# A two-layer encoder with 32 experts per layer: half as many, twice as long products per expert, and each expert's down product ahead of the next gate and up products in three rounds of four

## The chip, the core and the metric

The kernel runs on one core of a Trainium2 chip. The metric is the device time of one execution in microseconds (us), the median of several runs. A core has a matrix engine (TensorE, PE in the rows, its weight loads PEld), a vector engine (VectorE, DVE), a scalar engine (ScalarE, ACT), GpSimd (POOL) and a sync engine (SyncE, SP), which here issues the transfers from the chip's memory. All engines run side by side and wait for each other on semaphores. PSUM is the memory that TensorE writes to, in banks of 128 partitions by 512 floats.

## The reference

```python
for l in range(DEPTH):                       # 2 layers, 256 tokens, D_MODEL 1024
    x = x + concat(diff_attention, sparse_attention, mla)(rms_norm(x) @ w_in) @ w_out
    x = x + hier_moe(rms_norm(x))
return rms_norm(x)

def hier_moe(x):                             # 32 experts, 2 chosen per token
    gate, expert = top-2 experts of the best of 4 groups, for each token
    for each expert e, on its tokens xb:
        h = silu(xb @ w_gate[e]) * (xb @ w_up[e])      # 1024 x 512, 1024 x 512
        y = h @ w_down[e]                              # 512 x 1024
    return sum over a token's two experts of gate * y
```

All of it is float32. Every expert's three matrices, 6 MB together, are read from the chip's memory in each layer: 64 times 6 MB, which is most of what the kernel reads.

## The kernel before

One function, `trunk`, holds a program for each engine. In each of the two layers an attention part comes first, then a router, then the experts.

**The experts.** They come in `ROUNDS` = 4 rounds of `BODY` = 8. Each expert has `CAP` = 32 places for tokens. Four experts are a quad, and for each quad `tokens(q)` gathers the tokens by a product with a 0/1 matrix `pick` (line 1748), and ScalarE copies the result into `xg` in eight copies. One expert then is, in the words of this document:

- **P, the gate and up products** (`products`, `gate_up`, line 1766): 32 matrix products with 256 moving columns. The stationary operand has only 32 columns, so four products go side by side to the four groups of 32 columns of the array. The result is in `gu_ps`, 128 partitions by 256.
- ScalarE copies it to `h_rows` (`products_out`, `gu_read`).
- **T, the turning products** (`turned`, `turns`, lines 1777 and 1779): two transposes give h and two small products give the gate-weighted scatter matrix of this expert.
- ScalarE takes an exponential (`exponent`, line 819), and VectorE makes silu(gate) * up in four steps (`hidden`, lines 1230 to 1233, `hid_ready`), then four copies of the scatter matrix (line 1236, `pgt_read`).
- **D, the down product** (`down_of`, line 1789): 16 products of 256 columns into `tr`. ScalarE copies it to `y` (`y_out`, `wide_read`), and in the same place tells SyncE that the down matrix's buffer is free (`d_used`).
- **A, the scatter** (`add`, `scatter`, line 1799): 8 products of 256 columns, four side by side on four groups of 32 rows, add y to the sums of all tokens, which stand in the banks `pj` and `lg`.

TensorE runs its program strictly as written. Before, the order in a round is P(e), D(e-1), T(e), A(e-1).

**The transfers.** SyncE issues all large transfers in one fixed order. The experts' matrices have three places (`PLACES`), each 6 MB, and one late place for two experts of a layer. Experts 0 to 3 of a layer are loaded during the attention part, because their space is free then. Expert 4 goes to the place of expert 0 in pieces, expert 5 to that of expert 1, and from expert 6 on nearly each expert is one transfer of 6 MB (line 570, "all"), expert e into the place of expert e-3: 6 follows the expert 2, 7 the expert 4 (which had the place of 0), 8 the expert 5. Such a transfer waits for both `gu_used` and `d_used` of its place:

```python
if kind != "d":
    sp.wait_ge(gu_used[i], at(l, FILLS[i], uses(i, e)))
if kind != "gu":
    sp.wait_ge(d_used[i], at(l, FILLS[i], uses(i, e)))
if kind == "all":
    sp.dma_start(whole[i], experts_d[n]).then_inc(gu_full[i], 16)
```

So the transfer of expert 7 is issued when D(4) has ended. Behind the last expert of layer 0 come the attention weights of layer 1 (line 523), and TensorE starts that layer with line 1501.

## Time and profile before

| | us |
|---|---|
| median of 3 runs | 1163.73 (1161.87 to 1165.86) |
| the profiled execution | 1163.3 |
| its span, first to last instruction | 1161.4 |
| TensorE busy | 923.6 (80%) |
| VectorE, ScalarE busy | 417.7, 212.4 |
| chain that ended last: transfers, TensorE | 50%, 45% |

The profiled execution's own time lies 1.9 us above its span, and 0.4 us below the median of the runs. A line of a timeline gives the start, the length, the engine, the line of the kernel, what is written from what, the shapes and how many instructions are merged in it; in square brackets stands how long the engine had been idle and what it waited for. A float32 product counts as two matrix instructions, so P shows as x64 and D as x32.

### The profile page before, as it was taken

To read this page: it belongs to the slowest core of one execution; us is meant where nothing else is said; L and a number is where in the kernel's file an instruction comes from. 1 tells how busy PE (TensorE), PEld (TensorE's weight loads), DVE (VectorE), ACT (ScalarE), POOL (GpSimd) and SP (SyncE) were. 2 spreads that over 40 slices of the span, in tenths; PEclk is the share of its full clock that TensorE was granted. 3 is DMA by queue.
4 is the path that set the end of the run, shared out by engine and by line. 5 is a ranking of instruction groups with operands and counts; after the bars stand their busy time and mean duration, and the time that the engine had idled before them with its cause. 6 is when DMAs were issued, how large, how long until landed. Compare 5 with 4: busy or idle time off the path is not lost.

```text
span 1161.4 us, 22055 instructions
## 1 busy us (share of the span) xinstructions
PE 923.6 (80%) x9540; PEld 581.4 (50%) x9547; DVE 417.7 (36%) x1180; ACT 212.4 (18%) x623; POOL 16.3 (1%) x38
## 2 busy tenths in 40 slices
PE   9999999776766576668899999997585857566786
PEld 5876666453434343435468766654343524334443
DVE  3656554421231222222337464554222222222223
ACT  2234332010101010101112442310110101001012
POOL 1000000000000000000010000000000000000000
PEclk9999999987888889879999999999888978898799
DMA  7966499999999999999996466999999999999996
GB/s 305 414 239 246 192 392 437 421 430 433 431 431 433 431 429 428 432 424 417 424 393 239 163 240 250 402 432 432 430 431 431 429 433 433 428 430 425 421 421 276
DMA packets 28116, 445.04 MB, mean 383 GB/s; under 512 B 8944, under 2 KB 10352, under 8 KB 14832
## 3 DMA queue, kind: packets, MB, share of 16 engines
q1 hardware_dynamic: 27456, 443.49, 90.6%
q8 instruction: 78, 1.28, 0.4%
q10 hardware_dynamic: 560, 0.10, 0.0%
q14 instruction: 22, 0.18, 0.0%
HBM read 442.53 MB, written 1.05 MB: 382 GB/s over the span
## 4 chain that ended last, share of the span: by engine, by line
DMA 50%; PE 45%; issue 1%; DVE 1%; ACT 1%; SPq 1%; POOL 0%; POOLq 0%; ACTq 0%; DVEq 0%
DMA ring_xb<-in_experts 44%; PE pv L1766 12%; PE pj L1391 8%; PE tr L1789 5%; DMA arena<-in_experts 3%; DMA ring_xb<-in_w_in_chunks 3%; PE pj L1397 2%; PE pj L1501 2%; PE pj L1621 2%; PE pj L1596 1%; PE pj L1799 1%; PE pj L1630 1%; PE lg L1421 1%; PE tr L1431 1%; PE pv L1779 1%
## 5 line engine op out<-in xcount | busy, mean ns | idle before, releaser
L1766 PE MATMUL pv<-ring_xb,xT 128*32 128x256 f32 x3840 | 286.8, 459 | 174.1 <-DMA ring_xb<-in_experts 173.9
L1766 PEld LDWEIGHTS pv<-ring_xb,xT 128*32 128x32 f32 x3840 | 136.2, 127 | 312.3 <-DMA ring_xb<-in_experts 189.9
L1230 DVE TENSOR_SCALAR arena<-arena 128x128 f32<-128x128 f32 x64 | 14.6, 228 | 562.7 <-ACT arena L819 562.7
L1789 PE MATMUL tr<-ring_xb,arena 128*32 128x256 f32 x1920 | 115.4, 379 | 17.8 <-issue 15.1
L649 ACT ACTIVATE arena<-pv 128x256 f32<-128x256 f32 x64 | 24.6, 385 | 491.2 <-PE pv L1766 491.2
L1236 DVE COPY arena<-pv 32x256 f32<-32x256 f32 x256 | 105.5, 412 | 2.6
L1391 PE MATMUL pj<-xT,ring_xb 128*128 128x256 f32 x448 | 100.1, 381 | 0.0
L1789 PEld LDWEIGHTS tr<-ring_xb,arena 128*32 128x32 f32 x1920 | 63.9, 109 | 61.2 <-issue 19.6
L1391 PEld LDWEIGHTS pj<-xT,ring_xb 128*128 128x128 f32 x448 | 84.1, 190 | 13.1 <-issue 1.1
L1799 PE MATMUL pj<-arena 32*128 32x256 f32 x512 | 72.5, 399 | 6.7 <-ACT arena L649 5.4
L1748 PE MATMUL tr<-arena,rows 128*128 128x128 f32 x448 | 60.6, 300 | 15.2 <-issue 10.5
L1799 PE MATMUL lg<-arena 32*128 32x256 f32 x512 | 72.5, 400 | 0.0
L649 ACT ACTIVATE arena<-tr 128x256 f32<-128x256 f32 (+3 forms) x106 | 41.3, 407 | 151.1 <-PE tr L1789 128.9
L1748 PEld LDWEIGHTS tr<-arena,rows 128*128 128x128 f32 x448 | 58.0, 213 | 20.1 <-issue 14.7
L1231 DVE RECIPROCAL arena<-arena 128x128 f32<-128x128 f32 x64 | 61.0, 953 | 2.2
L1799 PEld LDWEIGHTS pj<-arena 32*128 32x128 f32 x512 | 44.5, 184 | 23.2 <-issue 19.7
L649 ACT ACTIVATE xT<-tr,gains 128x128 f32<-128x128 f32 x128 | 36.6, 369 | 75.7 <-PE tr L1748 73.5
L1799 PEld LDWEIGHTS lg<-arena 32*128 32x128 f32 x512 | 43.7, 184 | 0.0
L1779 PE MATMUL pv<-con,arena 128*32 128x128 f32 x256 | 40.0, 279 | 0.0
L1777 PE MATMUL pv<-con,arena 128*128 128x128 f32 x128 | 32.4, 335 | 9.5 <-ACT arena L649 9.5
L1777 PEld LDWEIGHTS pv<-con,arena 128*128 128x128 f32 x128 | 20.3, 207 | 37.3 <-issue 19.8
L649 ACT ACTIVATE arena<-pj 64x256 f32<-64x256 f32 (+2 forms) x48 | 21.0, 442 | 72.7 <-PE pj L1391 52.2
(228 smaller groups left out, 807.5 us busy)
## 6 DMA issues: line engine op xcount, KB each, us to landing
ring_xb<-in_experts SPq DMA_DIRECT2D x48, 6144.0 KB, 22.1
ring_xb<-in_experts SPq DMA_DIRECT2D x18, 2048.0 KB, 13.3
ring_xb<-in_experts SPq DMA_DIRECT2D x6, 4096.0 KB, 28.0
ring_xb<-in_w_in_chunks SPq DMA_DIRECT2D x10, 2048.0 KB, 19.5
ring_xb<-in_w_out_halves SPq DMA_DIRECT2D x4, 2048.0 KB, 29.9
arena<-in_experts SPq DMA_DIRECT2D x2, 4096.0 KB, 12.8
ring_xb<-in_experts SPq DMA_DIRECT2D x8, 1024.0 KB, 9.6
arena<-in_experts SPq DMA_DIRECT2D x4, 2048.0 KB, 37.9
```

The costliest lines, as they stand in the source:

```text
L649: return nc.scalar.activation(out, in_, ACT.Copy, **k)
L1231: own.link(v.reciprocal(e_neg, e_neg))
L1236: ins = v.tensor_copy(pgT[k * CAP:(k + 1) * CAP, b].rearrange("p t s -> p (t s)"), pgt_ps[0:CAP])
L1391: ins = mm(out, w[:, j], xT[:, j, :], start=(j == 0), stop=(j == KD - 1))
L1397: ins = mm(out, src[:, j, t * P:(t + 1) * P], weights(i, n)[:, j, c:c + m], start=(j == 0), stop=(j == KD - 1))
L1501: ins = mm(bank[:, 0:R5], xT_raw[:, j, t * P:(t + 1) * P], weights(0, n5)[:, j, :], start=(j == 0), stop=(j == KD - 1))
L1748: ins = mm(wide_ps[:, j * n:(j + 1) * n], rows[:, t, j * P:(j + 1) * P], pick[:, t, 0:n], start=(t == 0), stop=(t == TOK - 1))
L1766: ins = mm(gu_ps[i * CAP:(i + 1) * CAP, :], xg[:, j, c:c + CAP], w, start=(j == 0), stop=(j == KD - 1), tile_position=(0, i * CAP), skip_g ...
L1777: turn_(h_ps[:, c].rearrange("p h s -> p (h s)"), by_step[:, c], ident)
L1779: ins = mm(pgt_ps[0:CAP, t * P:(t + 1) * P], pgate[:, t, i, :], ident, start=True, stop=True, tile_position=(0, 0), skip_group_check=True)
L1789: ins = mm(tr[i * CAP:(i + 1) * CAP, 0, 0:SEQ], hid[:, b, k % 2, k // 2, :], rows_of[k][:, SEQ * i:SEQ * (i + 1)], start=(k == 0), stop=(k ...
L1799: ins = mm(sums[i][:, SEQ * t:SEQ * (t + 1)], pgT[r, b, t, :], y[r, :], start=False, stop=last, tile_position=(i * CAP, 0), skip_group_che ...
```

## The change

The number of products of one expert is halved and each is twice as long. In P the two halves of the moving matrix are no longer separate products: each has 512 columns, and the steps j of the sum go alternately to the even and the odd groups of columns, so that each of the four groups of 32 partitions holds half of a sum. The halves are added in T, by products with a 128 x 64 matrix of ones at the right places (`join`) in place of the transposes. D is built in the same way with 8 products of 512 columns, and A has 4 products of 512 columns on two groups of 64 rows. The copies to `h_rows` and `y` have 512 columns and not 256. The scatter matrix is turned once for a quad (two products of 128 columns), no longer for each expert.

In the rounds 0 to 2 the order becomes P(e), T(e), A(e-1), D(e), with `tokens(1)` before D(3). Round 3 keeps its order. The last expert's down matrix comes in five transfers and its last product, copy and scatter go in two halves. Four products that set the sums' banks to zero become one, three warm-up products at the start of layer 0 go, and ScalarE writes two of the four parts of the sums earlier.

```diff
-        acc = tuple(tuple(bank[:, :, SEQ * t:SEQ * (t + 1)] for bank in (pj, lg)) for t in range(TOK))
+        acc = tuple(tuple(bank[:, t] for bank in (pj, lg)) for t in range(TOK))
...
-        gu_ps = pv[:, 0, 0:HALF]
...
+        gu_ps = pv[:, 0]
+
+        h_ps = pv[:, 1, 0:2 * P].rearrange("p (k g s) -> p k g s", k=KE, g=2)
...
-        h_rows = take(HALF)
-        y = take(D_MODEL // QUAD)
+        h_rows = take(D_EXPERT)
+        y = take(D_MODEL // 2)
...
+
+        join = chosen.rearrange("p t e -> p (t e)")
...
                         elif e == LAST:
-                            for k in range(KE):
+                            for k in range(KE - 1):
                                 sp.dma_start(spare[k], down_v[n][:, k]).then_inc(last_in[k], 16)
+                            for side in range(2):
+                                there = slice(512 * side, 512 * side + 512)
+                                sp.dma_start(spare[KE - 1][:, there], down_v[n][:, KE - 1, there]).then_inc(last_in[KE - 1 + side], 16)
...
-                    if t == 1:
-                        open_sum(0, 1).then_inc(sums_open, 1)
-                        open_sum(1, 1).then_inc(sums_open, 1)
-                    else:
+                    if t == 0:
+                        open_sum(0, 1)
+                        open_sum(1, 1)
                         gate_exps(0)
...
-                        copy(y, tr[:, 0, 0:SEQ]).then_inc(wide_read, 1)
+                        copy(y, tr[:, 0]).then_inc(wide_read, 1)
+
+                    def last_y_out(e):
+
+                        act.wait_ge(lower_down, l + 1)
+                        copy(y[0:64], tr[0:64, 0]).then_inc(lower_y, 1)
+                        act.wait_ge(wide_done, at(r, WIDE, y_use(e)))
+                        act.sem_inc(d_used[place(m * BODY + e)], 1)
+                        copy(y[64:128], tr[64:128, 1]).then_inc(wide_read, 1)
...
-                        y_out(BODY - 2)
-                    products_out(BODY - 1)
-                    exponent(BODY - 1)
+                        if m < ROUNDS - 1:
+                            y_out(e)
                     if m == ROUNDS - 1:
                         y_out(BODY - 2)
-                    y_out(BODY - 1)
-
-                act.wait_ge(acc_done, at(l, 2 * TOK, 2 * TOK))
+                        last_y_out(BODY - 1)
...
+                def hidden(b, i, ready, turned):
+
+                    h = hid[:, b]
+                    own.link(v.tensor_scalar(h, h, 1.0, None, ALU.add))
+                    own.link(v.reciprocal(h, h))
+                    own.link(v.tensor_tensor(h, h_ps[:, :, 0, :], h, ALU.mult))
+                    v.tensor_tensor(h, h_ps[:, :, 1, :], h, ALU.mult).then_inc(ready, 1)
                     for k in range(KE):
-                        ins = v.tensor_copy(pgT[k * CAP:(k + 1) * CAP, b].rearrange("p t s -> p (t s)"), pgt_ps[0:CAP])
+                        ins = v.tensor_copy(pgT[k * CAP:(k + 1) * CAP, b].rearrange("p t s -> p (t s)"),
+                                            pgt_ps[i * CAP:(i + 1) * CAP])
                     ins.then_inc(turned, 1)
...
-                if l == 0:
-                    for _ in range(3):
-                        mm(lg[:, 0], zeros[:, 0:P], zeros[:, P:P + 512], start=True, stop=True)
...
-                        for i in range(4):
-                            w = both[:, j, D_EXPERT * (i // 2):D_EXPERT * (i // 2 + 1)].rearrange("p (d c) -> p d c", c=KE)[:, :, KE // 2 * (i % 2):KE // 2 * (i % 2) + KE // 2]
-                            ins = mm(gu_ps[i * CAP:(i + 1) * CAP, :], xg[:, j, c:c + CAP], w,
-                                     start=(j == 0), stop=(j == KD - 1), tile_position=(0, i * CAP),
-                                     skip_group_check=True)
+                        for g in range(2):
+                            i = 2 * g + j % 2
+                            ins = mm(gu_ps[i * CAP:(i + 1) * CAP, :], xg[:, j, c:c + CAP],
+                                     both[:, j, D_EXPERT * g:D_EXPERT * (g + 1)], start=(j < 2), stop=(j >= KD - 2),
+                                     tile_position=(0, i * CAP), skip_group_check=True)
                         if signal and j in REFILLS:
...
-                    by_step = h_rows.rearrange("q (p c) -> q c p", c=HALF // P)
-                    for c in range(HALF // P):
-                        turn_(h_ps[:, c].rearrange("p h s -> p (h s)"), by_step[:, c], ident)
+                def turns(quad):
+
+                    by_chunk = h_rows.rearrange("q (p k) -> q k p", k=KE)
+                    for k in range(KE):
+                        ins = mm(h_ps[:, k].rearrange("p g s -> p (g s)"), by_chunk[:, k], join, start=True, stop=True,
+                                 skip_group_check=True)
+                    if quad:
+                        for t in range(TOK):
+                            ins = mm(pgt_ps[:, t * P:(t + 1) * P], pgate[:, t].rearrange("p e s -> p (e s)"), ident,
+                                     start=True, stop=True, skip_group_check=True)
+                    return ins
+
+                def down_part(rows_of, b, k, side, bank):
...
+                        pe.wait_ge(last_in[k], 16 * (l + 1))
+                        for side in range(2):
+                            down_part(spare, b, k, side, side)
+                    pe.wait_ge(last_in[KE - 1], 16 * (l + 1))
+                    down_part(spare, b, KE - 1, 0, 0).then_inc(lower_down, 1)
+                    pe.wait_ge(last_in[KE], 16 * (l + 1))
+                    down_part(spare, b, KE - 1, 1, 1).then_inc(wide_done, 1)
+
+                def down(rows_of, b):
+
+                    for k in range(KE):
+                        for side in range(2):
+                            ins = down_part(rows_of, b, k, side, 0)
+                    return ins
+
+                def scatter_part(b, t, side, last):
+
+                    r = slice(64 * side, 64 * side + 64)
+                    return mm(acc[t][side], pgT[r, b, t, :], y[r, :], start=False, stop=last, tile_position=(64 * side, 0),
+                              skip_group_check=True)
+
...
                     for t in range(TOK):
...
-                        for i in range(4):
-                            ins = mm(tr[i * CAP:(i + 1) * CAP, 0, 0:SEQ], hid[:, b, k % 2, k // 2, :],
-                                     rows_of[k][:, SEQ * i:SEQ * (i + 1)], start=(k == 0), stop=(k == KE - 1),
-                                     tile_position=(0, i * CAP), skip_group_check=True)
-                    return ins
-
-                def scatter(b, last=False):
...
-                    for t in range(TOK):
-                        for i in range(4):
-                            r = slice(i * CAP, (i + 1) * CAP)
-                            ins = mm(sums[i][:, SEQ * t:SEQ * (t + 1)], pgT[r, b, t, :], y[r, :],
-                                     start=False, stop=last, tile_position=(i * CAP, 0), skip_group_check=True)
-                            if last and t == TOK - 1:
-                                ins.then_inc(acc_done, 1)
+                        for side in range(2):
+                            ins = scatter_part(b, t, side, False)
                     return ins
...
+                        scatter(e % 2)
+
+                    def down_and_add_last(e):
+
+                        pe.wait_ge(hid_ready, at(r, BODY, e + 1))
+                        pe.wait_ge(wide_read, at(r, READS, y_read(e) - 1))
+                        down_last(e % 2)
+                        pe.wait_ge(pgt_read, at(r, BODY, e + 1))
+                        pe.wait_ge(lower_y, l + 1)
+                        for side in range(2):
+                            if side == 1:
+                                pe.wait_ge(wide_read, at(r, READS, y_read(e)))
+                            for t in range(TOK):
+                                scatter_part(e % 2, t, side, True).then_inc(acc_done, 1)
...
                         tokens(0)
                         products(0)
                     turned(0)
-                    for e in range(1, BODY - 1):
-                        products(e)
-                        down_of(e - 1)
-                        turned(e)
-                        add(e - 1)
-                        if e == QUAD - 1:
-                            tokens(1)
-                    if m == ROUNDS - 1:
+                    if m < ROUNDS - 1:
+                        down_of(0)
+                        for e in range(1, BODY):
+                            products(e)
+                            turned(e)
+                            add(e - 1)
+                            if e == QUAD - 1:
+                                tokens(1)
+                            down_of(e)
+                        add(BODY - 1)
+                    else:
+                        for e in range(1, BODY - 1):
+                            products(e)
+                            down_of(e - 1)
+                            turned(e)
+                            add(e - 1)
+                            if e == QUAD - 1:
+                                tokens(1)
                         keep_warm(10)
-                    if m < ROUNDS - 1:
-                        down_of(BODY - 2)
-                        products(BODY - 1)
-                        turned(BODY - 1)
-                    else:
                         products(BODY - 1)
                         turned(BODY - 1)
                         keep_warm(4)
                         down_of(BODY - 2)
-                    add(BODY - 2)
-                    down_of(BODY - 1)
-                    add(BODY - 1)
...
+                        add(BODY - 2)
+                        down_and_add_last(BODY - 1)
```

**TensorE, layer 0, from the turning products of expert 0 to the scatter of expert 0** (`pv` is written by P and T, `tr` by D, `pj` and `lg` by A). Before:

```order
L1777 MATMUL pv<-con,arena 128x128 x2
L1779 MATMUL pv<-con,arena 32x128 x2
L1766 MATMUL pv<-ring_xb,xT 32x256 x32
L1789 MATMUL tr<-ring_xb,arena 32x256 x16
L1777 MATMUL pv<-con,arena 128x128 x2
L1779 MATMUL pv<-con,arena 32x128 x2
L1799 MATMUL pj<-arena 128x256 x2
```

The same place of the change:

```order
L1791 MATMUL pv<-arena 128x64 x4
L1795 MATMUL pv<-con,arena 128x128 x2
L1802 MATMUL tr<-ring_xb,arena 32x512 x8
L1780 MATMUL pv<-ring_xb,xT 32x512 x16
L1791 MATMUL pv<-arena 128x64 x4
L1826 MATMUL pj<-arena 128x512
```

D(0), line 1789 before and 1802 now, has moved from behind P(1) to ahead of it, right behind the turning products of its own expert.

**TensorE, layer 0, from the scatter of expert 2 to the down product of expert 3** (line 1748 before and 1762 now are the gather of the second quad). Before:

```order
L1799 MATMUL lg<-arena 128x256 x2
L1748 MATMUL tr<-arena,rows 128x128 x16
L1766 MATMUL pv<-ring_xb,xT 32x256 x32
L1789 MATMUL tr<-xT,arena 32x256 x4
L1789 MATMUL tr<-arena 32x256 x4
L1789 MATMUL tr<-lowrank,arena 32x256 x4
```

The same place of the change:

```order
L1826 MATMUL lg<-arena 128x512
L1762 MATMUL tr<-arena,rows 128x128 x16
L1802 MATMUL tr<-xT,arena 32x512 x2
L1802 MATMUL tr<-arena 32x512 x2
L1802 MATMUL tr<-lowrank,arena 32x512 x2
L1802 MATMUL tr<-arena 32x512 x2
L1780 MATMUL pv<-ring_xb,xT 32x512 x16
```

D(3) now stands between the gather and P(4), and it writes the same banks `tr` as the gather.

**SyncE, layer 0, the transfers of experts 4 to 23** as one piece of the difference (4096 is half a gate and up matrix or a down matrix, 8192 gate and up, 12288 a whole expert):

```order
 L507 DMA ring_xb<-in_experts 128x4096
 L575 DMA ring_xb<-in_experts 128x8192
-L580 DMA ring_xb<-in_experts 128x4096 x2
+L583 DMA ring_xb<-in_experts 128x4096 x2
 L570 DMA ring_xb<-in_experts 128x12288 x18
```

Only a line number differs: the transfers keep their order, sizes and waits.

## Rows read from the trace of the kernel before

**Rows 1.** Stretches: length, PE, PEld, DVE, ACT, POOL busy, PEclk, DMA share, GB/s.

```profile
205.00:575.00 370.00, 260.50 (x3282) 153.06 (x3288) 101.10 (x259) 40.93 (x126) 0.00 (x0) 0.86 1.00 428
582.00:732.00 150.00, 148.82 (x741) 107.03 (x746) 79.76 (x260) 49.48 (x142) 5.91 (x10) 1.00 0.66 260
```

**Rows 2.** Chain that ended last: start, length, what; two places of layer 0.

```profile
202.78 19.51 DMA ring_xb<-in_experts
...
543.63 38.29 DMA ring_xb<-in_w_in_chunks
581.96 6.17 PE pj L1501 x16
```

**Rows 3.** Timeline of TensorE, layer 0, experts 0 to 7.

```profile
162.09 0.50 PE L1777 MATMUL pv<-con,arena 128*128 128x128 f32 x2 [0.60 <-ACT arena L649]
166.49 2.10 PE L1789 MATMUL tr<-ring_xb,arena 128*32 128x256 f32 x32
185.74 3.84 PE L1748 MATMUL tr<-arena,rows 128*128 128x128 f32 x32
189.51 3.83 PE L1766 MATMUL pv<-ring_xb,xT 128*32 128x256 f32 x64
197.07 3.83 PE L1766 MATMUL pv<-ring_xb,xT 128*32 128x256 f32 x64
...
207.82 5.43 PE L1766 MATMUL pv<-ring_xb,xT 128*32 128x256 f32 x64 [3.13 <-DMA ring_xb<-in_experts]
...
222.34 3.86 PE L1766 MATMUL pv<-ring_xb,xT 128*32 128x256 f32 x64 [2.05 <-DMA ring_xb<-in_experts]
```

**Rows 4.** Timeline of all engines, D(4), T(5) and the steps behind it.

```profile
200.72 1.91 PE L1789 MATMUL tr<-ring_xb,arena 128*32 128x256 f32 x32
...
202.56 0.50 PE L1777 MATMUL pv<-con,arena 128*128 128x128 f32 x2
202.78 0.33 SPq L570 DMA_DIRECT2D ring_xb<-in_experts  x1
...
203.00 0.62 PE L1779 MATMUL pv<-con,arena 128*32 128x128 f32 x4
...
203.66 0.28 ACT L819 ACTIVATE arena<-pv 128x128 f32<-128x128 f32 x1 [0.49 <-PE pv L1779]
...
205.62 0.29 DVE L1233 TENSOR_TENSOR arena<-pv,arena 128x128 f32<-128x128 f32 x1
```

**Rows 5.** Whole-expert transfers one by one: issue, and time from issue to landing.

```profile
L570 SPq DMA_DIRECT2D ring_xb<-in_experts x1: 328/328/328, 202.8 to 202.8; - x1
...
DMA to landing us min/median/max: 19.5/19.5/19.5
...
L570 SPq DMA_DIRECT2D ring_xb<-in_experts x1: 328/328/328, 777.6 to 777.6; - x1
...
DMA to landing us min/median/max: 18.9/18.9/18.9
...
L474 SPq DMA_DIRECT2D ring_xb<-in_experts x1: 328/328/328, 630.7 to 630.7; - x1
...
DMA to landing us min/median/max: 18.4/18.4/18.4
```

**Rows 6.** Timeline of other places: operations of the changed sizes, and both ends.

```profile
135.91 3.70 PE L1630 MATMUL pj<-ring_xb,xT 128*128 128x512 f32 x8
...
140.25 1.06 PE L1679 MATMUL pv<-wr,arena 128*128 128x40 f32 x8
...
145.72 0.60 ACT L649 ACTIVATE arena<-pj 128x512 f32<-128x512 f32 x1 [1.76 <-PE pj L1641]
...
189.62 1.15 ACT L649 ACTIVATE xT<-tr,gains 128x128 f32<-128x128 f32 x4 [0.64 <-PE tr L1748]
...
5.50 1.49 PE L1489 MATMUL lg<-zeros 128*128 128x512 bf16 x3
...
15.10 0.34 DVE L932 TENSOR_SCALAR arena<-con,rms 128x128 f32<-128x128 f32 x1 [0.84 <-POOL rms L613]
```

More of the change, by code:

```diff
@@ L867, in _ @@
                                 act.wait_ge(o_wide, i * 2 + 2)
[L868 removed]
+                                copy(y, tr[:, 0]).then_inc(o_wide_read, 1)
                     gathered(0)
[L870 to L872 removed]
+                    for e in range(BODY):
                         products_out(e)
[L874 removed]
+                        if m == ROUNDS - 1 and 0 < e < BODY - 1:
+                            y_out(e - 1)
                         exponent(e)
@@ L1699, in gather_first @@
                     return ins
-                def zero_sum(i):
-                    mm(sums[i], zeros[:, 0:P], zeros[:, P:P + 512], start=True, stop=False,
-                       skip_group_check=True).then_inc(sums_zeroed, 1)
                 out_upper(1, 1)
@@ L1732, in keep_warm @@
                     for _ in range(n):
-                        mm(sums[0], zeros[:, 0:P], zeros[:, P:P + 512], start=False, stop=False,
+                        mm(pj[:, 0].rearrange("p (n c) -> p n c", n=KE), zeros, spread(zeros, 1, KE), start=False, stop=False,
                            skip_group_check=True)
@@ new lines, in down_part, with down_last @@
+                def down_part(rows_of, b, k, side, bank):
+                    i = 2 * side + k % 2
+                    return mm(tr[i * CAP:(i + 1) * CAP, bank], hid[:, b, k, :], rows_of[k][:, 512 * side:512 * side + 512],
+                              start=(k < 2), stop=(k >= KE - 2), tile_position=(0, i * CAP), skip_group_check=True)
+                def down_last(b):
+                    for k in range(KE - 1):
+                        pe.wait_ge(last_in[k], 16 * (l + 1))
[5 more added lines that the diff above has]
+                    down_part(spare, b, KE - 1, 1, 1).then_inc(wide_done, 1)
```

116 lines of the change are left out of this document (53 added, 63 removed).

## The prediction

> **What bounds the kernel now.** I read the busy time by stretch first. From 205 to 575 us the transfers have a share of 1.00 at 428 GB/s while TensorE is busy for 260.5 of 370 us [rows 1]: in the experts' part the memory stream sets the pace, and TensorE has nearly a third of the time to spare. Between the experts of layer 0 and those of layer 1 it is the other way round: TensorE is busy for 148.82 of 150 us, the transfers for 0.66. The chain that ended last shows the seams [rows 2]: layer 1 starts with line 1501 when the attention weights land at 581.96, behind the last expert in the queue. So the time is the attention part, plus the bytes of the experts at a fixed rate, plus a tail, plus **any moment at which the queue of transfers is empty**. Faster or slower products inside the saturated stretch are worth nothing, unless they hold back a transfer so long that the queue runs dry.
>
> The place where it nearly does so is the start of each layer's experts. There four experts are already loaded, TensorE has no wait for data, and the transfers follow its pace. The timeline shows P starting every 7.56 us (189.51 to 197.07) [rows 3]. At 202.78, when D(4) ends, the 6 MB of expert 7 are issued [rows 4]; they land 19.5 us later, at 222.3 [rows 5], which TensorE is waiting for. Its layer 1 twin is issued at 777.6 and lands after 18.9. How much of this is queueing? A whole expert that is issued into an empty queue (630.7, line 474) lands after 18.4 us [rows 5]. So expert 7 finds the queue all but empty already: **the cushion is 19.5 - 18.4 = 1.1 us in layer 0 and 18.9 - 18.4 = 0.5 in layer 1.** Every microsecond by which D(4) is later, above these, is a hole in the stream which nothing can fill later, because from there to the next attention part the share is 1.00.
>
> The Trainium skill weighs this otherwise: "DMA: Bandwidth & Descriptors", section on the anatomy of one DMA, fits a transfer as some 2.0 us plus its bytes over 436 GB/s, 16.4 us for 6.29 MB, which would make the cushion 3.1 and 2.5 us and the forecast about 4 us lower. The trace differs (18.4), and its row is for this very transfer.
>
> **The change part by part, at the start of the experts.** I follow TensorE from the end of P(0) to the end of D(4), first with prices.
>
> P: 64 matrix instructions of 256 columns take 3.83 us [rows 3]; the same columns in half as many instructions. Eight of 512 columns one after the other take 3.70 (line 1630) [rows 6], and each of the four column groups has eight, so P takes 3.7. That is the whole gain of longer products: 0.1.
>
> Wait before T: 0.60 at expert 0 [rows 3], with a copy of 256 columns. The copy of 512 takes 0.60 in place of about 0.38 (145.72) [rows 6]: 0.8. Until now only expert 0 paid this, since D(e-1) stood there; now every expert pays it.
>
> T: eight instructions with full stationary operands and only 40 columns take 1.06 (line 1679) [rows 6], as long as T now, 202.56 to 203.62 [rows 4]. The new T has eight with 64 columns: 1.06. The quads' first experts, 0 and 4, have four more instructions, at 3.84 / 32 = 0.12 each (the gather) [rows 3]: 1.5.
>
> From the end of T to D: T(5) ends at 203.62, the fourth step of `hidden` at 205.91 [rows 4], so 2.3. These steps have the same number of elements. Until now P(e+1) lay over them and they cost TensorE nothing. Now only A(e-1) does. A is four products of 512 columns, on two groups of rows side by side: two, that is four instructions, of 3.70 / 8 = 0.46 each, 1.9 (before 1.15). It fits inside the 2.3; the longer A is hidden, and expert 0, without an A, idles through the whole.
>
> D: as P, no shorter: 1.9, and the next P starts 1.8 behind D's start.
>
> So an expert takes 3.7 + 0.8 + 1.06 + 2.3 + 1.8 = 9.7 us and not 7.56. Moving D forward takes one P from the way to D(4), but puts five waits on it. Step by step in layer 0: P(0) ends at 161.5 (0.60 before T(0) at 162.09) [rows 3]. D(0) starts 0.8 + 1.5 + 2.3 later, at 166.1, P(1) at 167.9, P(2) at 177.6, P(3) at 187.3, ending at 191.0. T(3) ends at 192.9, A(2) at 194.8. The gather of the second quad (3.84) [rows 3] ends at 198.6. D(3) writes the same banks, so it waits for the last four copies of the gather, 1.15 [rows 6]; before, P(4) stood there and hid them. D(3) starts at 199.9, P(4) at 201.7, D(4) at 201.7 + 3.7 + 0.8 + 1.5 + 2.3 = 210.0, and it ends at 211.9. Before it ended at 202.63. **D(4) is 9.2 us later.** The order of SyncE's transfers is the same, so expert 7 is issued at 212.0 and lands at 230.4, after 222.3: a hole of 8.1 us. In layer 1 the same steps give 9.2 - 0.5 = 8.7.
>
> Other transfers at this place: that of expert 5 waits for P(1), which ends at 171.6 and not about 166.8. Even if all of these 4.8 us ran through to expert 6 (in TensorE at 207.82 [rows 3], then 212.6), expert 7, 14.5 behind it, would land at 227.1, ahead of the 230.4 that D(4) sets. So it is not added. Expert 8 is issued when D(5) ends, near 221.6, while expert 7 still flows for 8 us: queue full again. From there on D earlier in each round only lengthens the queue, and a share of 1.00 cannot grow: 0.
>
> **The ends.** The three warm-up products take 1.49 us [rows 6]; the first layer then waits for a scale that VectorE only writes at 15.10 + 0.34 [rows 6], so I take 0, and up to -1.3 if that cover is thinner than it looks. The sums' zeroing stands between waits: 0. The last expert: its last down product is one pair of 512 columns, 0.9 and not 0.64, its copy 0.2 longer, its scatter 0.7 longer, and against these one half of all goes earlier and lies under the transfer: +0.3, between -1 and +1.1. In layer 0 that tail lies under the attention weights' landing.
>
> **Sum.** The profiled execution took 1163.3, 0.4 below the median. 1163.3 + 8.1 + 8.7 + 0.3 = 1180.4; I forecast 1180 for the median, 1.4% above now.
>
> **The rivals.** *Forecast, chance 0.60*: a hole of 6 to 10 us per layer, 1175 to 1184.
> *The hole is smaller, 0.14*: if P, the waits and the way through ScalarE and VectorE come out a microsecond shorter per expert, D(4) is 5 us late and the sum is 1163.3 + 4 + 4.5 = 1172. For it speaks only that five latencies add up their errors; against it, that each is read from a row.
> *The clock falls too, 0.10.* P took 5.43 after 3.13 us idle and 3.86 after 2.05 idle [rows 3]; the 1.6 between them is a first part at the lower of the clock's two levels, 1.2 and not 2.4 GHz (the granted mean from 205 to 575 is 0.86 [rows 1]). The stop before D(0) is 2.3 us. If the clock falls there and once more, that is 1.6 to 3.2 per layer: 1183 to 1187. The Trainium skill, "TensorE: Matmul & The Clock Gate", part 1, calls the lower level the default that activity lifts; the trace agrees, 5.43 against 3.86.
> *No difference, 0.07*: the hole is taken up because expert 7 has a longer cushion than one transfer's row says. It would need 9 us where I read 1.1: 1163.
> *Faster, 0.05*: the stream never runs dry, which needs D(4) no later than 1.1 us, that is experts at 7.7 us each. Then the front (-1.3), the zeroing (-0.4 a layer) and a tail at its better end (-1) remain: 1160.
> *A is not side by side, 0.04*: eight instructions in a row take 3.7 [rows 6] and stick out of the 2.3 by 1.4 at experts 1, 2 and 4 and delay the gather by 1.8: 6 a layer, 1192. For it: no row shows two groups of 64 rows. Against it: A now runs four abreast, and so do P and D.
>
> Faster than now by over 0.3% (about what a measurement of this kernel can tell from no change): 0.05. Within 0.3%: 0.07. Slower: 0.88. The range runs from the smaller hole, 1171, to the fallen clock, 1187.
>
> **What would show it.** Right, if the timeline after shows P of experts 1 to 3 every 9.7 us with waits of 0.8 before T and some 0.4 before D; expert 7's transfer issued 9 us later relative to P(0), landing 18.4 us behind its issue; the transfers' share below 1 for some 6 us just before it, in both layers; and from there to the last expert an unchanged time. Wrong, if the transfers stay at 1.00 through the start, or if the stretch behind expert 7 gets shorter, which would mean that the present stream has losses that I don't see.

## The result and the profile after

The changed kernel takes 1202.9 us (1199.94 to 1207.37) beside 1163.2 (1161.87 to 1165.86): 1.0339 times as long, interval 1.0319 to 1.0358. The forecast was 1180, between 1171 and 1187. It is slower, as forecast, but by 40 us and not by 17. The profiled execution took 1204.6, with a span of 1202.7.

Busy time by stretch of the changed kernel. The columns are: stretch, its length, busy us of TensorE, weight loads, VectorE, ScalarE and GpSimd, then the granted clock, the share of the transfers and GB/s.

```profile
165.00:185.00 20.00, 17.07 (x112) 6.50 (x112) 6.96 (x16) 2.07 (x4) 0.00 (x0) 0.83 0.71 288
200.00:235.00 35.00, 31.60 (x213) 15.28 (x214) 14.06 (x39) 5.83 (x15) 0.00 (x0) 0.91 0.66 276
780.00:825.00 45.00, 39.61 (x264) 20.46 (x260) 15.16 (x39) 7.58 (x19) 0.00 (x0) 0.96 0.76 318
```

The kernel before at the start of layer 0:

```profile
165.00:185.00 20.00, 20.00 (x313) 12.17 (x306) 8.97 (x23) 3.09 (x9) 0.00 (x0) 1.00 1.01 430
200.00:230.00 30.00, 21.85 (x306) 12.45 (x298) 14.08 (x40) 3.14 (x9) 0.00 (x0) 0.94 1.00 426
```

The hole in the stream is there, but in two parts, and larger: 0.29 of 20 us and 0.34 of 35 us make 17.7 us without transfer at the start of layer 0, where the kernel before had none. (From 185 to 200 us the share is 1.0 in both.) TensorE's timeline of the changed kernel at the same place, against [rows 3, 4]:

```profile
161.84 2.08 PE L1791 MATMUL pv<-arena 128*128 128x64 f32 x8 [0.80 <-ACT arena L652]
166.74 3.64 PE L1802 MATMUL tr<-ring_xb,arena 128*32 128x512 f32 x16 [2.31 <-issue]
170.12 4.67 PE L1780 MATMUL pv<-ring_xb,xT 128*32 128x512 f32 x32
175.60 2.08 PE L1791 MATMUL pv<-arena 128*128 128x64 f32 x8 [0.80 <-ACT arena L652]
177.61 0.69 PE L1826 MATMUL pj<-arena 64*128 64x512 f32 x1
...
179.99 1.92 PE L1802 MATMUL tr<-ring_xb,arena 128*32 128x512 f32 x16 [0.40 <-issue]
181.71 3.64 PE L1780 MATMUL pv<-ring_xb,xT 128*32 128x512 f32 x32
...
200.62 1.06 PE L1826 MATMUL pj<-arena 64*128 64x512 f32 x1
...
201.62 4.46 PE L1762 MATMUL tr<-arena,rows 128*128 128x128 f32 x32
...
209.12 3.64 PE L1780 MATMUL pv<-ring_xb,xT 128*32 128x512 f32 x32
213.55 2.08 PE L1791 MATMUL pv<-arena 128*128 128x64 f32 x8 [0.79 <-ACT arena L652]
...
219.28 2.26 PE L1802 MATMUL tr<-ring_xb,arena 128*32 128x512 f32 x16
```

Line 1791 is T, 1802 D, 1780 P, 1826 A, 1762 the gather. D(4) ends at 219.28 + 2.26 = 221.54, which is 18.9 us later than the 202.63 of before. Three things differ from the forecast's steps: each T has 2.08 us and not 1.06; D(0) and P(1), behind the first stop of 2.31 us, take 3.64 and 4.67 and not 1.92 and 3.64 (the granted clock is 0.83 from 165 to 185 us); and A(2) (single instructions of 1.06 and not 0.59), the gather, A(3) and D(4) are slow too (4.46 for the gather, 2.26 for D(4); the granted clock is 0.59 from 199 to 202 us and 0.60 from 216 to 219, so it stood mostly at the lower of its two levels, 1.2 GHz). SyncE issues expert 7 right behind D(4), and the transfer lands after 17.8 us, at 239.5:

```profile
221.71 0.33 SPq L570 DMA_DIRECT2D ring_xb<-in_experts  x1
...
ring_xb<-in_experts SPq DMA_DIRECT2D x1, 6144.0 KB, 17.8
```

The other new loss stands at the end of each layer. TensorE's timeline of the changed kernel from the last expert's T on:

```profile
1180.40 2.08 PE L1791 MATMUL pv<-arena 128*128 128x64 f32 x8 [0.80 <-ACT arena L652]
1182.31 1.65 PE L1748 MATMUL pj<-zeros 128*128 128x512 bf16 x4
1183.89 2.94 PE L1802 MATMUL tr<-ring_xb,arena 128*32 128x512 f32 x16
```

The same place of the kernel before:

```profile
1143.13 0.51 PE L1777 MATMUL pv<-con,arena 128*128 128x128 f32 x2 [0.59 <-ACT arena L649]
...
1145.45 1.93 PE L1789 MATMUL tr<-ring_xb,arena 128*32 128x256 f32 x32 [0.28 <-DMA ring_xb<-in_experts]
```

From T(31) to the end of the span it was 1161.4 - 1143.13 = 18.3 us and is now 1202.7 - 1180.40 = 22.3: 4.0 us more. T is 1.0 of it (2.08 and not 1.06), and D(30), at 2.94 and not 1.93, another 1.0. Before, D(30) waited 0.28 us for its transfer; now it starts right behind T and four products of zeros. Layer 0 ends in the same way; before, it was:

```profile
568.82 0.51 PE L1777 MATMUL pv<-con,arena 128*128 128x128 f32 x2 [0.58 <-ACT arena L649]
...
581.96 0.64 PE L1501 MATMUL pj<-ring_xb,rows 128*128 128x440 f32 x1 [0.39 <-DMA ring_xb<-in_w_in_chunks]
```

T(31) of layer 0 now starts at 586.03, 17.2 us later, close to the 17.7 of the holes, and from there to layer 1's first product it is 17.2 us and not 13.1, 4.1 more. So layer 1 starts at 603.25 instead of 581.96 [rows 2], 21.3 later.

### The profile page after: what moved, and what is told of

It is laid out like the page before. It is cut to its first block, busy times and chain, and to the rows that moved or that the text cites. A ratio compares the mean times of both kernels' runs of the same rounds, so it can differ in the third digit from the quotient of the medians.

```text
span 1202.7 us, 15268 instructions
## 1 busy us (share of the span) xinstructions
PE 1045.8 (87%) x6146; PEld 561.2 (47%) x6146; DVE 423.9 (35%) x1182; ACT 240.9 (20%) x625; POOL 15.8 (1%) x38
## 4 chain that ended last, share of the span: by engine, by line
PE 61%; DMA 30%; issue 3%; ACT 3%; DVE 2%; SPq 0%; ACTq 0%; POOLq 0%; DVEq 0%; POOL 0%
DMA ring_xb<-in_experts 30%; PE pv L1780 12%; PE pj L1415 8%; PE tr L1802 7%; PE pj L1826 6%; PE pv L1791 6%; PE tr L1762 4%; PE pj L1421 2%; ACT arena L652 2%; PE pj L1522 2%; PE pj L1642 2%; PE pj L1617 1%; PE pj L1651 1%; PE lg L1445 1%; PE pj L1748 1%
## 5 line engine op out<-in xcount | busy, mean ns | idle before, releaser
L1780 PE MATMUL pv<-ring_xb,xT 128*32 128x512 f32 x1920 | 234.0, 629 | 55.4 <-DMA ring_xb<-in_experts 55.2
L1791 PEld LDWEIGHTS pv<-arena 128*128 128x128 f32 x512 | 124.3, 327 | 99.0 <-ACT arena L652 97.3
L1791 PE MATMUL pv<-arena 128*128 128x64 f32 x512 | 133.4, 404 | 41.7 <-ACT arena L652 41.7
L1826 PE MATMUL pj<-arena 64*128 64x512 f32 x256 | 159.3, 753 | 9.0 <-ACT arena L652 9.0
L1780 PEld LDWEIGHTS pv<-ring_xb,xT 128*32 128x32 f32 x1920 | 64.3, 116 | 212.3 <-issue 125.8
L1826 PE MATMUL lg<-arena 64*128 64x512 f32 x256 | 159.7, 754 | 0.0
L1802 PE MATMUL tr<-ring_xb,arena 128*32 128x512 f32 x960 | 129.4, 661 | 28.8 <-issue 21.0
L652 ACT ACTIVATE arena<-tr 128x512 f32<-128x512 f32 (+4 forms) x108 | 56.1, 537 | 270.3 <-PE tr L1802 248.1
L1415 PEld LDWEIGHTS pj<-xT,ring_xb 128*128 128x128 f32 x448 | 84.1, 190 | 13.1 <-issue 1.1
L1826 PEld LDWEIGHTS pj<-arena 64*128 64x128 f32 x256 | 51.2, 220 | 62.7 <-issue 58.5
L1762 PEld LDWEIGHTS tr<-arena,rows 128*128 128x128 f32 x448 | 53.7, 200 | 19.5 <-issue 15.3
L1826 PEld LDWEIGHTS lg<-arena 64*128 64x128 f32 x256 | 51.2, 220 | 0.5 <-issue 0.5
L826 ACT ACTIVATE arena<-pv 128x128 f32<-128x128 f32 x64 | 17.8, 278 | 138.0 <-PE pv L1791 95.6
## 6 DMA issues: line engine op xcount, KB each, us to landing
ring_xb<-in_w_in_chunks SPq DMA_DIRECT2D x10, 2048.0 KB, 21.3
```

Source lines behind the costliest of these rows:

```text
L652: return nc.scalar.activation(out, in_, ACT.Copy, **k)
L1415: ins = mm(out, w[:, j], xT[:, j, :], start=(j == 0), stop=(j == KD - 1))
L1762: ins = mm(wide_ps[:, j * n:(j + 1) * n], rows[:, t, j * P:(j + 1) * P], pick[:, t, 0:n], start=(t == 0), stop=(t == TOK - 1))
L1780: ins = mm(gu_ps[i * CAP:(i + 1) * CAP, :], xg[:, j, c:c + CAP], both[:, j, D_EXPERT * g:D_EXPERT * (g + 1)], start=(j < 2), stop=(j >= KD ...
L1791: ins = mm(h_ps[:, k].rearrange("p g s -> p (g s)"), by_chunk[:, k], join, start=True, stop=True, skip_group_check=True)
L1802: return mm(tr[i * CAP:(i + 1) * CAP, bank], hid[:, b, k, :], rows_of[k][:, 512 * side:512 * side + 512], start=(k < 2), stop=(k >= KE - 2 ...
```

## The experiments

All ratios are to the kernel before, which gave 1163.3 to 1164.2 beside them. Theory A: the time follows the end of D(4) at each layer's start, through the issue of expert 7, and D(4) is late by the order, by slow T and by the fallen clock. The rivals: the clock or the products' work itself sets the time everywhere; or the new order costs in all rounds.

**1. Is the hole a hole?** Before, with 20 products of zeros ahead of D(4) in round 0, and nothing else:

```diff
                         products(e)
+                        if m == 0 and e == 5:
+                            keep_warm(20)
                         down_of(e - 1)
```

> The kernel before with 20 products of zeros between P(5) and D(4) of round 0 in each layer, 20 x 0.216 = 4.3 us on TensorE and nothing else. If a late D(4) opens a hole that nothing fills later, with cushions of 1.1 and 0.5 us: 1163 + 3.2 + 3.8 = 1170. If the stream recovers: 1163.

Measured: 1171.2 (1170.95 to 1171.4), ratio 1.0062 (1.0045 to 1.0079). TensorE's timeline, and the two stretches of 200 to 235 and 780 to 825 us:

```profile
200.66 4.49 PE L1733 MATMUL pj<-zeros 128*128 128x512 bf16 x20
205.08 1.93 PE L1789 MATMUL tr<-ring_xb,arena 128*32 128x256 f32 x32
...
200.00:235.00 35.00, 26.80 (x322) 14.00 (x314) 12.42 (x37) 3.13 (x9) 0.00 (x0) 0.90 0.92 387
780.00:825.00 45.00, 32.06 (x398) 18.98 (x399) 18.00 (x56) 4.74 (x15) 0.00 (x0) 0.92 0.92 391
```

D(4) ends at 207.01, 4.4 later. TensorE has over 100 us to spare in the saturated stretch of a layer [rows 1], and still 4.4 us at this one place in each layer cost 7.0 in all. That agrees with the forecast's cushions (4.4 - 1.1 + 4.4 - 0.5 = 7.2), though the interval, 5.2 to 9.2 us, doesn't tell them from somewhat smaller or larger ones. The transfers stand still for 0.08 x 35 = 2.8 us.

**2. The order alone**: the products of before in the new order.

```diff
-                    for e in range(1, BODY - 1):
-                        products(e)
-                        down_of(e - 1)
-                        turned(e)
-                        add(e - 1)
...
+                    if m < ROUNDS - 1:
+                        down_of(0)
+                        for e in range(1, BODY):
+                            products(e)
+                            turned(e)
+                            add(e - 1)
+                            if e == QUAD - 1:
+                                tokens(1)
+                            down_of(e)
+                        add(BODY - 1)
```

> The kernel before with the new order alone (P, T, A, D in rounds 0 to 2), its products and its last expert as they were. If the hole in the transfers behind a late D(4) is the cause and the order makes it: the experts at the start come every 9.6 us (3.83 + 0.6 + 1.06 + 2.3 + 1.8), D(4) ends 7 to 10 us later than before, and the time is 1163 plus 6 to 9 per layer, 1176 to 1182. If the order costs nothing and the long products are the whole loss: 1163.

Measured: 1178.2 (1177.24 to 1179.28), ratio 1.0120 (1.0103 to 1.0137).

```profile
165.35 3.54 PE L1786 MATMUL tr<-ring_xb,arena 128*32 128x256 f32 x32 [2.31 <-issue]
...
208.94 1.93 PE L1786 MATMUL tr<-ring_xb,arena 128*32 128x256 f32 x32 [1.24 <-issue]
...
165.00:185.00 20.00, 17.04 (x236) 10.17 (x236) 6.45 (x16) 2.10 (x6) 0.00 (x0) 0.91 0.87 357
200.00:235.00 35.00, 28.62 (x448) 17.86 (x439) 15.87 (x44) 3.91 (x11) 0.00 (x0) 1.00 0.91 382
```

D(4) ends at 210.87, 8.2 later, as expected. D(0) stands behind the same stop of 2.31 us as in the changed kernel and takes 3.54 us and not 1.93: 1.6 of the 8.2 are the slower clock.

**3. The products alone**: the changed kernel with the old order everywhere.

> The changed kernel with the old order in all rounds; the new products, copies and the last expert in halves stay. By the prices measured after the change (P 3.5, D 1.75, T 2.1, A 2.0) an expert takes 9.4 us at the start and not 7.56, D(4) ends some 9 us later than in the kernel before, expert 7 lands 8 us later in each layer, and the ends of the layers cost 3 to 4 more each: 1185 to 1189. If the order is the whole loss: 1163 to 1166.

Measured: 1181.6 (1181.31 to 1186.93), ratio 1.0151 (1.0134 to 1.0168).

```profile
163.94 2.08 PE L1805 MATMUL pv<-arena 128*128 128x64 f32 x8 [0.80 <-ACT arena L652]
...
211.03 1.90 PE L1816 MATMUL tr<-ring_xb,arena 128*32 128x512 f32 x16
```

That is 3 to 7 us less than I had expected, and the execution profiled here was a long one, 1186.9. So nearly half of the loss comes without any change of order, from longer T and A: in the old order nothing lies beside them. Each part alone makes D(4) 8.2 us later (this execution began its experts 2.1 us later than the changed kernel, T(0) at 163.94 and not 161.84, which is taken off), both together 18.9. Together they cost more than the sum of the two (14.0 + 17.4 = 31.4 of 39.7 us): above the cushion of 1.1 us the single delays are 7.1 and 7.1 and the joint one 17.8, which is 3.6 a layer or 7.2 in all. The cushion is spent once and not twice, and the clock falls further (below).

**4. What T costs**: the changed kernel with the copied products laid out so that T's stationary operands are contiguous. The work and the order are the same.

```diff
-                        copy(h_rows, gu_ps).then_inc(gu_read, 1)
+                        copy(h_rows.rearrange("q (k p) -> q k p", k=KE), gu_ps.rearrange("q (p k) -> q k p", k=KE)).then_inc(gu_read, 1)
...
-                    by_chunk = h_rows.rearrange("q (p k) -> q k p", k=KE)
+                    by_chunk = h_rows.rearrange("q (k p) -> q k p", k=KE)
```

> The changed kernel, but the copy to h_rows puts the four chunks one behind the other, so that T's stationary operand is read from adjacent elements and no longer with a step of 16 bytes. If that step makes T's weight loads take 0.23 and not 0.11 us each, T falls from 2.08 to some 1.1 us, D(4) comes 5 us earlier in each layer and each layer's end 1 us: 1203 - 12 = 1191. If T is slow for its 64 moving columns or the float32 loads as such: 1203.

Measured: 1182.4 (1181.27 to 1183.52), ratio 1.0161 (1.0144 to 1.0178): half of the loss is gone, 20.5 us with one access pattern. The weight loads of T (shortest, median and longest in ns) first in the changed kernel:

```profile
L1791 PEld LDWEIGHTS pv<-arena x512: 307/329/332, 161.8 to 1182.0; 128*128 128x128 f32 x171
```

then with contiguous operands, and there too the timeline and the stretches at the start of layer 0:

```profile
L1791 PEld LDWEIGHTS pv<-arena x512: 186/192/192, 161.8 to 1160.9; 128*128 128x128 f32 x171
...
165.74 2.90 PE L1802 MATMUL tr<-ring_xb,arena 128*32 128x512 f32 x16 [2.31 <-issue]
168.34 4.45 PE L1780 MATMUL pv<-ring_xb,xT 128*32 128x512 f32 x32
173.59 1.10 PE L1791 MATMUL pv<-arena 128*128 128x64 f32 x8 [0.79 <-ACT arena L652]
...
195.68 3.84 PE L1762 MATMUL tr<-arena,rows 128*128 128x128 f32 x32
...
210.91 1.92 PE L1802 MATMUL tr<-ring_xb,arena 128*32 128x512 f32 x16 [0.40 <-issue]
...
165.00:185.00 20.00, 17.28 (x124) 7.09 (x126) 6.37 (x17) 2.95 (x6) 0.00 (x0) 0.91 0.79 324
200.00:235.00 35.00, 30.43 (x244) 12.44 (x244) 16.09 (x44) 5.71 (x13) 0.00 (x0) 1.00 0.85 356
```

I had expected 12 us less than 1203 and got 20.5 (23.0 between the two profiled executions). D(4) ends at 212.83, 8.7 earlier. Five T are 5.0 of it. The other 3.7 are clock: D(0) and P(1) together 1.0, the gather 0.6, D(4) 0.3, and A(2) and A(3), of whose instructions half or more took up to 1.06 and not 0.59 in the changed kernel, some 1.8. The rest of the gain is at the layers' ends: from T(31), here at 1160.11, to the end of the span 1179.8 - 1160.11 = 19.7 and not 22.3. Twice 8.7 and twice 2.6 make 22.6, beside the 23.0 of the profiled executions.

**5. What the first stop costs**: the changed kernel, and the one of 4, with ten products of zeros in the wait ahead of D(0).

```diff
                     if m < ROUNDS - 1:
+                        if m == 0:
+                            pe.wait_ge(sums_open, l + 1)
+                            keep_warm(10)
                         down_of(0)
```

> The changed kernel, with ten warm-up products (bfloat16 zeros, they add nothing to the sums) ahead of D(0) in the first round of each layer, where TensorE otherwise stands still for 2.3 us. Ten such products took 2.33 us at a layer's end in the changed kernel's trace, so they should about fill the wait. Theory A (the stop lets the granted clock fall and D(0) and P(1) pay for it, 3.64 and 4.67 us in place of 1.92 and 3.64): D(0) and P(1) are back at 1.9 and 3.6, D(4) ends 2.7 us earlier, and each layer is as much shorter: about 1197.5. Rival B (the clock is low there because of what stands before the stop, or the slow start of the layer isn't what sets the transfer): no change, 1203. Rival C: the fillers stick out and cost their own time, 1203 to 1206.

> The changed kernel with contiguous stationary operands of the turning products (1182.4) and, in addition, the ten warm-up products ahead of D(0) in each layer's first round. D(0) took 2.90 and P(1) 4.45 us there, against 1.92 and 3.64 at full clock: theory A expects 1.8 us less per layer, 1178.8. Rival B: no change, 1182.4.

Measured: 1197.5 (1196.68 to 1200.14), ratio 1.0287 (1.0272 to 1.0302), and 1178.5 (1178.37 to 1179.47), ratio 1.0128 (1.0111 to 1.0144). The first kernel's timeline:

```profile
164.25 2.32 PE L1748 MATMUL pj<-zeros 128*128 128x512 bf16 x10
166.73 1.92 PE L1802 MATMUL tr<-ring_xb,arena 128*32 128x512 f32 x16 [0.15 <-issue]
168.44 3.64 PE L1780 MATMUL pv<-ring_xb,xT 128*32 128x512 f32 x32
...
216.48 1.93 PE L1802 MATMUL tr<-ring_xb,arena 128*32 128x512 f32 x16
```

D(0) starts at the same time, but it and P(1) run at the full clock, 2.75 us less together. D(4) ends 3.1 us earlier, and the time falls by 5.4 and by 3.9: work that computes nothing makes the kernel faster, by 2.7 and 1.95 us a layer. With the long T the fillers didn't end the slow stretches: A(0), which had run at the full clock, now had instructions of 1.06 us, while A(2) and the gather were back at 0.59 and 3.84. With the short T all of them ran at the full clock.

**6. The order in the later rounds**: the changed kernel with the old order in round 0 only.

> The changed kernel, with the old order of the down products in the first round of each layer, and the new order in the second and third. Theory A (the order costs only at the start of a layer's experts, where it delays D(4) and with it the transfer of expert 7; later the transfers set the pace): the same time as with the old order everywhere, 1181.6, give or take 2. Rival B (the waits of the new order cost in the later rounds too): between 1185 and 1203. Rival C (an earlier down product in the later rounds sends transfers earlier and brings something): under 1178.

Measured: 1183.5 (1180.9 to 1185.41), ratio 1.0166 (1.0146 to 1.0186). The interval overlaps that of 3. The order in rounds 1 and 2 is worth nothing that can be measured, in either direction; a difference of less than some 3 us would not show.

**7. Contiguous T and the old order** (the edits of 3 and 4 together)

> The long products with the old order everywhere (1181.6) and, in addition, the copied products laid out so that the stationary operands of the turning products are contiguous. If a turning product of 2.08 us (eight loads 0.23 apart) becomes 1.10 as it did with the new order, the five ahead of D(4) save 5 us of a hole of about 7 per layer, and at a layer's end another 1 to 2.6 us come back: 1166 to 1170. Rival: the turning products' length isn't what delays D(4) in the old order, since other engines' work lies beside it: 1178 or more. If the hole is really what costs, the idle time of the transfers at the start must be near 2 us per layer, and the time at or above the kernel before (1164).

Measured: 1168.5 (1167.47 to 1168.85), ratio 1.0039 (1.0025 to 1.0053).

```profile
204.02 1.90 PE L1816 MATMUL tr<-ring_xb,arena 128*32 128x512 f32 x16
...
200.00:235.00 35.00, 28.06 (x204) 9.88 (x204) 17.53 (x49) 4.41 (x9) 0.00 (x0) 0.90 0.93 390
```

D(4) is 3.3 us late, mainly because A takes 2.0 us and not 1.15 where nothing lies beside it; the hole is 0.07 x 35 = 2.4 us.

**8. Mend the hole and not its cause**: expert 7's transfer in two, the gate and up matrices behind P(4), only the down matrix behind D(4).

```diff
-        return order + [("all", e) for e in range(AHEAD + 2, last)]
+        return order + [("all", 6), ("gu", 7), ("d", 7)]
...
-D_LOADS = {1: 1, 2: 3, AHEAD: 1, AHEAD + 1: 1,
+D_LOADS = {1: 1, 2: 3, AHEAD: 1, AHEAD + 1: 1, 7: 1,
```

> The changed kernel, with the transfer of expert 7 in each layer split: its gate and up matrices (4 MB) are issued as soon as P(4) has been copied out, and only its down matrix (2 MB) waits for D(4). If the second hole of the stream exists only because the whole transfer stands behind D(4), it shrinks: P(4) ends at 212.7 and D(4) at 221.5 in the changed kernel's trace, 8.8 us apart. But expert 7 would then land near 231, and expert 8's transfer waits for D(5), near 232: a new hole of 1 to 3 us. So 6 to 8 us less per layer: 1187 to 1191. Rival (the start costs time through something else, so that the issue time of this transfer doesn't matter): 1203.

> Long products, old order, contiguous stationary operands (1168.5), with the transfer of expert 7 split in the same way. P(4) ends 10 us ahead of D(4) there, and the hole is 3.0 and 2.9 us in the two layers: it should vanish, and the time should be that of the kernel before, 1163.5, or less if the longer products and the shorter ends are worth anything (down to 1161). Rival (what remains against the kernel before, 5.0 us, isn't the hole): 1168.

> The changed kernel with contiguous stationary operands and the fillers ahead of D(0) (1178.5), with the transfer of expert 7 split. The second hole is about 5 us per layer there and should go, and no new one should come (D(5) ends at 220.8, expert 7 would land near 223). The first hole, 2.4 us, stays: 1169 to 1170. Rival: no change, 1178.

> The kernel before with the transfer of expert 7 split. Its stream has no hole at this place, so an earlier issue only lengthens the queue: 1163.5, no change. Rival (the short transfer queue at this place costs something that the share of busy time doesn't show): 1160 to 1162.

| kernel with the split | median us | without it | ratio to before |
|---|---|---|---|
| changed | 1195.5 | 1202.9 | 1.0280 (1.0264 to 1.0295) |
| contiguous T, old order | 1162.9 | 1168.5 | 0.9993 (0.9984 to 1.0002) |
| contiguous T, fillers, new order | 1171.2 | 1178.5 | 1.0075 (1.0061 to 1.0090) |
| before | 1163.4 | 1163.3 | 1.0000 (0.9991 to 1.0009) |

The split kernel of 7 has lost its whole difference to the kernel before, so that was the hole. The third kernel kept its first hole (share 0.88 from 165 to 185 us) and came out at 1171.2 where I had expected 1169 to 1170. The changed kernel gained 7.4 and not 12 or more. SyncE's queue there, and two stretches of 15 us:

```profile
212.83 0.33 SPq L575 DMA_DIRECT2D ring_xb<-in_experts  x1
221.63 0.33 SPq L583 DMA_DIRECT2D ring_xb<-in_experts  x1
232.30 21.57 SPq L570 DMA_DIRECT2D ring_xb<-in_experts  x3
...
205.00:220.00 15.00, 12.89 (x82) 6.13 (x84) 3.38 (x9) 3.05 (x9) 0.00 (x0) 0.89 0.79 320
225.00:240.00 15.00, 12.97 (x80) 7.02 (x80) 6.21 (x16) 2.35 (x5) 0.00 (x0) 1.00 0.80 319
```

The stall moved on: expert 7 is early, and the queue runs dry before expert 8, which waits for D(5) until 232.3. I had expected that, but at 1 to 3 us in all; the stretch around the issue of expert 7 still has 0.21 x 15 = 3.2 us without transfer, and the new one ahead of expert 8 has 3.0. No version beats the kernel before by more than the noise. Where the holes are gone the share of the transfers is 1.00 from 200 to 235 us, and all versions move the same bytes within 0.1% (444.6 and 445.0 MB); that the bytes then set the time is my reading of it.

**All of it in one table.** D(4)'s end in layer 0, how much later than before it is, and the idle time of the transfers, (1 - share) x length of the stretches 165 to 185 and 200 to 235 us:

| kernel | D(4) ends | later | later - 1.1 | idle | median |
|---|---|---|---|---|---|
| before | 202.6 | 0 | 0 | 0 | 1163.5 |
| contiguous T, old order | 205.9 | 3.3 | 2.2 | 2.4 | 1168.5 |
| 20 zero products | 207.0 | 4.4 | 3.3 | 2.8 | 1171.2 |
| order alone | 210.9 | 8.2 | 7.1 | 5.8 | 1178.2 |
| contiguous T, fillers | 211.1 | 8.5 | 7.4 | 7.6 | 1178.5 |
| contiguous T | 212.8 | 10.2 | 9.1 | 9.5 | 1182.4 |
| products alone | 212.9 | 8.2 (2.1 taken off) | 7.1 | 6.9 | 1181.6 |
| changed, fillers | 218.4 | 15.8 | 14.7 | 14.4 | 1197.5 |
| changed | 221.5 | 18.9 | 17.8 | 17.7 | 1202.9 |

Twice "later - 1.1" gives the time above 1163.5 within about 1 us in the five rows without the long T. In the three rows with it ("products alone" and the last two) 4 to 5 us more were measured, and there the ends of the layers are longer too.

## Why the prediction was right or wrong

**The mechanism was right**, and it is shown, not only argued: the time follows D(4)'s end, above a cushion of about 1 us (table; experiment 1), the saturated rest gives nothing back, and the order in the later rounds costs nothing that can be measured (6). A ran side by side and was hidden (177.61 to 179.6, forecast 1.9), P took 3.64 (3.7), the wait before T 0.80 (0.8), the way from T's end to D 2.31 (2.3), the next P came 1.7 behind D (1.8). That expert 5's transfer is "not added" was right as well: it is issued 7.9 us later and makes the first of the two holes, but both together are what D(4) dictates (17.7 against 17.8).

**The step that failed most is T.** "The new T has eight with 64 columns: 1.06" took the price from eight products with full stationary operands at line 1679 [rows 6]. There the stationary operand is contiguous. The new T reads every fourth float32 of `h_rows`, a step of 16 bytes, and each load takes 0.33 us and not 0.19, and comes 0.23 behind the one before it. With the same instructions on contiguous operands T took 1.10: the row was right for the operation and wrong for the access pattern. The T of before read with a step of 8 bytes, which cost little, though these were transposes and not products, so this row is not quite the same instruction. Its loads in the kernel before:

```profile
L1777 PEld LDWEIGHTS pv<-con,arena x128: 194/208/223, 162.1 to 1143.2; 128*128 128x128 f32 x128
```

The Trainium skill, "Advanced Engine Details and Errata", section Memory Cachelines, has the rule that I didn't weigh: SBUF is read in lines of 16 bytes, and an access pattern needs two hits in a line to hide the access. All three rows agree with it: one hit a line 329 ns, two 208, four 192. By that rule the new T should have been priced as an unknown with a range, and it was worth 20.5 us in all.

**The fallen clock** was a rival at 0.10 and it came true beside the forecast's hole, not in its place. "1.6 to 3.2 per layer" was the right size for D(0) and P(1), 2.75 in layer 0. But the clock fell again at A(2) and A(3), which cost another 2.7 there with the gather and D(4) (experiment 4), so that all of it was 5.4, more than the rival had. I priced it from P after waits for transfers [rows 3], and then left it out of the sum, although the sum itself put a stop of 2.3 us there, between the 2.05 that had cost P nothing and the 3.13 that had cost it 1.6 in those rows. The later part came only with the long T; with the short T all of these ran at the full clock. By what way the long T brings the clock down isn't shown.

**The ends**: "+0.3" measured 4.0 per layer, of which 2.6 are T and the clock behind it, since contiguous T leaves 1.4. I had said that in layer 0 "that tail lies under the attention weights' landing". It did not: before, TensorE had waited only 0.39 us for that landing, so no more than this could be hidden. The chain that ended last runs through TensorE from D(30) at 589.16 to layer 1's first product at 603.25 without a transfer in it, where [rows 2] ended in one:

```profile
586.03 2.08 PE pv L1791 x8
...
589.16 3.36 PE tr L1802 x16
...
603.25 5.91 PE pj L1522 x16
```

**The sum, by runs.** With T contiguous and the wait filled, the changed kernel took 1178.5; that is the kernel which the forecast's sum of 1180.4 describes. The clock at D(0) and P(1) adds 3.9 (1182.4), the access pattern of T 20.5 (1202.9). One per-expert term had a wrong price and the clock had none; the first was multiplied by five experts and two layers, at the one place where nothing is hidden.

What stays open: the order alone has 1.3 us less idle time in the transfers than its D(4) says. The last 1.4 us of each end were not taken apart (A on 64 rows, the copies in two halves). The kernels with contiguous T are also some 2 to 3 us faster than the delays of D(4) and twice this 1.4 add up to: with the split and the old order there is no hole, the end is 19.7 and not 18.3, and the time is still 1162.9. So the long products give something back elsewhere; where isn't shown.

## What to carry to other kernels

Where one queue bounds a kernel, look for the one instruction that feeds it when it is shortest, and count every microsecond up to there at full price; in the saturated part behind it the same change cost nothing here. The tail of a layer, where nothing is hidden either, is priced in the same way. A delay put there on purpose (experiment 1) measures the cushion in one run. Price an operation from a row with the same access pattern as well as the same shape: the step of the stationary operand doubled T here. Where a sum puts a new stop into TensorE's program, the slower clock behind it belongs in the sum; filling the stop with products that add nothing took it away here with the short T, and moved part of it to a later place with the long one.

## What the runs showed of the hardware

- A weight load of a float32 128 x 128 operand takes 192 ns contiguous, 208 with a step of 8 bytes (in transposes) and 329 with one of 16 bytes; eight products on contiguous loads take 1.10 us, and 2.08 on those with the step of 16 bytes.
- Behind a stop of 2.31 us in TensorE the next 16 and 32 instructions took 3.64 and 4.67 us in place of 1.92 and 3.64, and with products of zeros in the stop they didn't. How much they lose differs between kernels with the same stop: 2.90 and 4.45 with the short T ahead of it, and 3.54 and 3.85 in place of 1.93 and 3.83 with the products of before. What sets it isn't shown.
- Into an empty queue a 6 MB transfer took 17.8 us here, 0.6 less than the row on which the cushion rested [rows 5]. That row had a transfer of 0.5 MB issued right behind it (at 631.0), which may be the difference; with 17.8 the cushion in layer 0 would have been read as 19.5 - 17.8 = 1.7. The Trainium skill, "DMA: Bandwidth & Descriptors", section Anatomy of one DMA, would have 16.4 for it by its fit, an estimate; it gives that fit for transfers issued through GpSimd, a condition that the forecast left out, and these are SyncE's. The trace shows more in both cases.
- Splitting a 6 MB transfer into 4 and 2 cost nothing where the queue is full (1.0000, 0.9991 to 1.0009).
